# Thirteen late input blocks per layer split into two rounded halves, and the gate tables dealt out anew

## The reference

```
q = (h @ wq).reshape(B, S, H, PEER_QDIM)
s1, s2 = the two halves of q against k1, k2        # 128 scores each
v1, i1 = lax.top_k(s1, K);  v2, i2 = lax.top_k(s2, K)
top_s, pos = lax.top_k(v1 + v2 of all pairs, K)
gates = jax.nn.softmax(top_s, axis=-1)
act = jax.nn.gelu(jnp.einsum('td,tkd->tk', xc, u[ec]), approximate=False)
y = jnp.einsum('tk,tkd->td', act * gc, v[ec])
```

## Time and profile before

| | |
|---|---|
| median of three executions | 1907.43 us (1905.97 to 1910.97) |
| the profiled execution | 1905.52 us |
| its span, first to last instruction | 1903.6 us |
| mean granted TensorE clock in it | 0.997 |
| TensorE, VectorE, ScalarE, GpSimd busy | 98%, 83%, 52%, 23% of the span |
| DMA | 547.98 MB, mean 288 GB/s |

### The profile page before, as it was taken

One profiled execution on the slowest core, in us unless ns is written; L12 is line 12 of the kernel. 1 busy time (PEld: TensorE's weight loads), 2 busy tenths in 40 slices (PEclk: granted clock), 3 DMA queues, 4 the chain that ended last, 5 costly groups with the idle time before them and its releaser, 6 DMA issues.

```text
span 1903.6 us, 35537 instructions
## 1 busy us (share of the span) xinstructions
PE 1859.9 (98%) x13294; PEld 1803.7 (95%) x13294; DVE 1587.8 (83%) x3192; ACT 989.2 (52%) x1933; POOL 438.6 (23%) x368
## 2 busy tenths in 40 slices
PE   6999999999999999999999999999999999999998
PEld 6899989999999999999988898999999999999998
DVE  7788889989688598898888978898976776888897
ACT  4478455621455455555555775555115554555554
POOL 0000000022455334333100001000226552334330
PEclk9999999999999999999999999999999999999999
DMA  8766765699989899999867746656998888999994
GB/s 340 251 247 214 277 213 185 203 323 362 318 311 336 302 343 358 346 352 346 309 238 265 257 161 211 229 189 220 361 359 275 300 297 303 349 347 356 350 354 157
DMA packets 152160, 547.98 MB, mean 288 GB/s; under 512 B 18080, under 2 KB 18720, under 8 KB 151520
## 3 DMA queue, kind: packets, MB, share of 16 engines
q1 hardware_dynamic: 115168, 412.08, 61.0%
q0 software_dynamic: 36864, 134.23, 19.8%
HBM read 540.74 MB, written 1.57 MB: 285 GB/s over the span
## 4 chain that ended last, share of the span: by engine, by line
PE 74%; DVE 13%; DMA 7%; ACT 3%; issue 2%; POOL 1%; SPq 0%; ACTq 0%; DVEq 0%
PE ps L1717 24%; PE ps L2023 13%; PE ps L2019 9%; PE ps L1601 5%; DVE w_lo L1008 4%; DMA raw<-in_v 4%; PE ps L1597 3%; PE ps L1598 3%; PE ps L1594 3%; PE ps L1988 2%; PE ps L1759 1%; ACT w_hi L651 1%; DMA raw<-in_u 1%; DVE big L1474 1%; PE ps L1915 1%
## 5 line engine op out<-in xcount | busy, mean ns | idle before, releaser
L651 ACT CAST w_hi<-raw 128x1024 fp32r<-128x1024 f32 x460 | 483.6, 1051 | 516.0 <-PE ps L2019 163.1
L1008 DVE TENSOR_TENSOR w_lo<-raw,w_hi 128x1024 fp32r<-128x1024 f32 x460 | 562.2, 1223 | 121.3 <-ACT w_hi L651 118.9
L1717 PE MATMUL ps<-big,raw 128*128 128x192 f32 x3104 | 516.7, 327 | 0.6 <-DMA raw<-in_u 0.5
L1717 PEld LDWEIGHTS ps<-big,raw 128*128 128x128 f32 x3104 | 502.9, 190 | 1.8 <-DMA raw<-in_u 1.6
L614 POOL DMA_INDIRECT hot<-in_v,spare x128 | 199.4, 1558 | 365.5 <-DVE big L1474 314.7
L2023 PE MATMUL ps<-h_both,w_hi 128*128 128x384 f32 x960 | 191.4, 341 | 0.6 <-ACT w_hi L651 0.5
L2023 PE MATMUL ps<-p_both,w_hi 128*128 128x384 f32 x960 | 191.0, 340 | 0.3 <-ACT w_hi L651 0.3
L2023 PEld LDWEIGHTS ps<-h_both,w_hi 128*128 128x128 f32 x960 | 162.9, 189 | 1.6 <-issue 1.0
L2023 PEld LDWEIGHTS ps<-p_both,w_hi 128*128 128x128 f32 x960 | 162.8, 189 | 0.6 <-ACT w_hi L651 0.5
L1597 PE MATMUL ps<-h_both,w_hi 128*128 128x256 f32 (+1 forms) x648 | 160.3, 286 | 1.4 <-ACT big L656 1.2
L1474 DVE SCALAR_TENSOR_TENSOR big<-hot,spare,big 128x1024 f32<-128x1024 f32 x126 | 161.1, 1278 | 0.0
(11 more groups left out here) (247 smaller groups left out, 2918.9 us busy)
## 6 DMA issues: line engine op xcount, KB each, us to landing
raw<-in_u SPq DMA_DIRECT2D x256, 512.0 KB, 5.0
raw<-in_v SPq DMA_DIRECT2D x256, 512.0 KB, 6.2
raw<-in_win SPq DMA_DIRECT2D x104, 512.0 KB, 4.6
hot<-in_ada SPq DMA_DIRECT2D x62, 512.0 KB, 4.9
big<-in_ada SPq DMA_DIRECT2D x34, 512.0 KB, 7.4
raw<-in_wq SPq DMA_DIRECT2D x32, 512.0 KB, 5.0
raw<-in_wout SPq DMA_DIRECT2D x16, 512.0 KB, 4.5
big<-in_decay SPq DMA_DIRECT2D x2, 1536.0 KB, 8.0
```

The source lines that it names most:

```text
L651: nc.scalar.copy(w_hi[:, j % 2, :], raw[:, j, :]).then_inc(hi_ready, covered(n))
L1008: tt(w_lo[:, j % 2, :], raw[:, j, :], w_hi[:, j % 2, :].bitcast(F32), ALU.subtract).then_inc(lo_ready, covered(n))
L1717: last = mm(bank(E[m % 2])[:, 0:DENSE], raw[:, j, P * k:P * (k + 1)], h_full[:, k, :], start=(k == 0), stop=(k == KC - 1))
```

## The change

Of the plain blocks 98 to 127 every second one from 98 to 122 (`LATE_U`, 13 per layer, 26 in all) is now split. Its high part goes to bank 6 or 7, and its low half is added by one matmul at the end of the plain block that follows. The Gelu of a late block runs after the next block is done, together with that block's own, and so the two products of VectorE stand together. Plain blocks among them use banks 1 and 0 in turn. Apart from that, GpSimd makes 3 of the 8 tables of each gate, ScalarE 3 and VectorE 2, at all 24 gates of a layer.

```diff
--- before.py
+++ after.py
@@ -92,7 +92,7 @@
 V_COPIES = 5
 SWAPS = 4
 BATCH = 8
-POOL_TOK, ACT_TOK = 2, 4
+POOL_TOK, ACT_TOK = 3, 3
 GATE_SCALE = 1024.0
 N_SPARSE = 64
 DENSE = SEQ - N_SPARSE
@@ -153,7 +153,9 @@
 PLAIN_U = range(N_HALF, N_U)
 assert len(FIRST_U) % LONG == 1 and LONG % 4 == 0 and N_HALF % 4 == 3
 V_PLAIN = 2
-RAW = LIFTED | {N_BLOCKS * l + B_U + m for l in range(DEPTH) for m in range(N_HALF, N_U + V_PLAIN)}
+LATE_U = range(98, 124, 2)
+LATE_BANK, MIXED_BANK = (6, 7), (1, 0)
+RAW = LIFTED | {N_BLOCKS * l + B_U + m for l in range(DEPTH) for m in range(N_HALF, N_U + V_PLAIN) if m not in LATE_U}
 V_PAIRS = (N_V - V_PLAIN) // 2
 EU = (1, 6, 7, 0)
 
@@ -437,6 +439,16 @@
         def home(m):
 
             return (M if m < 2 or C_AQ <= m < C_AQ + 2 else E)[m % 2]
+
+        def late_bank(m):
+
+            return bank(LATE_BANK[m // 2 % 2])
+
+        def plain_bank(m):
+
+            if LATE_U[0] < m <= LATE_U[-1] + 1:
+                return bank(MIXED_BANK[m // 2 % 2])
+            return bank(E[(m + (m > LATE_U[-1])) % 2])
         block = ctx.enter_context(nc.Block())
 
         @block.sync
@@ -949,18 +961,24 @@
                     if n + 2 not in RAW:
                         round_hi(n + 2, (n + 2) % RING)
                     act.wait_ge(block_done, n + 1)
+                    if m in LATE_U:
+                        nc.scalar.copy(p_both[:, 1, 0:1, 0:nd], late_bank(m)[:, nd:2 * nd]).then_inc(ulow_copied, 1)
                     if m in FIRST_U:
                         nc.scalar.copy(p_both[:, 1, m % 2, 0:nd], bank(EU[m % 4])[:, nd:2 * nd]).then_inc(ulow_copied, 1)
                     if m - 1 in FIRST_U:
                         nc.scalar.activation(acts[:, m - 1:m, 0:nd], bank(EU[(m - 1) % 4])[:, 0:nd], ACT.Gelu).then_inc(out_taken, 1)
+                    if m - 1 in LATE_U:
+                        act.wait_ge(producted, l * N_PROD + m - M_PROD - 2)
+                        nc.scalar.activation(acted[:, (m - 1) % 2:(m - 1) % 2 + 1, 0:nd], late_bank(m - 1)[:, 0:nd], ACT.Gelu
+                                             ).then_inc(out_taken, 1)
                     if m < M_PROD:
                         o = acts[:, m:m + 1, 0:nd]
                     else:
-                        if m >= M_PROD + 2:
+                        if m >= M_PROD + 2 and m not in LATE_U:
                             act.wait_ge(producted, l * N_PROD + m - M_PROD - 1)
                         o = acted[:, m % 2:m % 2 + 1, 0:nd]
-                    if m not in FIRST_U:
-                        nc.scalar.activation(o, bank(E[m % 2])[:, 0:nd], ACT.Gelu).then_inc(out_taken, 1)
+                    if m not in FIRST_U and m not in LATE_U:
+                        nc.scalar.activation(o, plain_bank(m)[:, 0:nd], ACT.Gelu).then_inc(out_taken, 1)
                     if m == 2:
                         copy_scores(3)
                     if m in (TOK_COPY_AT, TOK_COPY_AT + 1):
@@ -1512,9 +1530,10 @@
                         us.link(stt(gate16[:, 0, :], turned_gate, GATE_SCALE, gate16[:, 1, :], ALU.mult, ALU.subtract))
                         ts(neg[:], rt[:, 2, 0:DENSE].rearrange("p (b t) -> p b t", t=BATCH)[:, :, POOL_TOK:POOL_TOK + ACT_TOK], -2.0, None,
                            ALU.mult).then_inc(choices_ready, 1)
-                    if m > M_PROD:
-                        product(m - 1, weighed)
-                        products += 1
+                    for at in (m - 2, m - 1):
+                        if at >= M_PROD and m == (at + 2 if at in LATE_U else at + 1):
+                            product(at, weighed)
+                            products += 1
                     for b in range(N_GATE):
                         if gate_after(b) == m - 1:
                             weigh(b, products)
@@ -1703,7 +1722,7 @@
                     last = mm(o[:, 0:DENSE], w_lo[:, s, P * k:P * (k + 1)], h_hi[:, k, 0:DENSE], start=False, stop=False,
                               skip_group_check=True)
                 if after_wide:
-                    pe.wait_ge(ulow_copied, l * len(FIRST_U) + m - FIRST_U[0])
+                    pe.wait_ge(ulow_copied, l * (len(FIRST_U) + len(LATE_U)) + m - FIRST_U[0])
                     last = add_half(j - 1)
                 last.then_inc(block_done, 1)
 
@@ -1714,7 +1733,7 @@
                 pe.wait_ge(raw_in[j], (n - j) * (16 // RING) + 16)
                 pe.wait_ge(out_taken, l * EV + E_U + m - behind + 1)
                 for k in range(KC):
-                    last = mm(bank(E[m % 2])[:, 0:DENSE], raw[:, j, P * k:P * (k + 1)], h_full[:, k, :], start=(k == 0),
+                    last = mm(plain_bank(m)[:, 0:DENSE], raw[:, j, P * k:P * (k + 1)], h_full[:, k, :], start=(k == 0),
                               stop=(k == KC - 1))
                 if then:
                     last = then()
@@ -1990,13 +2009,39 @@
 
                 def last_half():
 
-                    pe.wait_ge(ulow_copied, (l + 1) * len(FIRST_U))
+                    pe.wait_ge(ulow_copied, l * (len(FIRST_U) + len(LATE_U)) + len(FIRST_U))
                     return add_half(FIRST_U[-1])
+
+                def late_half(m):
+
+                    pe.wait_ge(ulow_copied, l * (len(FIRST_U) + len(LATE_U)) + len(FIRST_U) + LATE_U.index(m) + 1)
+                    return mm(late_bank(m)[:, 0:DENSE], ident_r, p_both[:, 1, 0, 0:DENSE], start=False, stop=True,
+                              skip_group_check=True)
+
+                def project_late(m):
+
+                    s, n = m % 2, l * N_BLOCKS + B_U + m
+                    pe.wait_ge(hi_ready, n + 1)
+                    pe.wait_ge(out_taken, l * EV + E_U + m - 3)
+                    o = late_bank(m)
+                    for k in range(KC):
+                        mm(o[:, 0:2 * DENSE].rearrange("p (a t) -> p a t", a=2), w_hi[:, s, P * k:P * (k + 1)],
+                           h_both[:, :, k, 0:DENSE], start=(k == 0), stop=False, skip_group_check=True)
+                    pe.wait_ge(lo_ready, n + 1)
+                    for k in range(KC):
+                        last = mm(o[:, 0:DENSE], w_lo[:, s, P * k:P * (k + 1)], h_hi[:, k, 0:DENSE], start=False, stop=False,
+                                  skip_group_check=True)
+                    last.then_inc(block_done, 1)
 
                 pe.wait_ge(hfull_ready, KC * (l + 1))
                 for m in PLAIN_U:
                     behind = m - FIRST_U[-1]
-                    project_plain(l, m, 3 if behind < 3 else 2, last_half if behind == 1 else None)
+                    if m in LATE_U:
+                        project_late(m)
+                    elif m - 1 in LATE_U:
+                        project_plain(l, m, 4, lambda: late_half(m - 1))
+                    else:
+                        project_plain(l, m, 3 if behind < 3 else 2, last_half if behind == 1 else None)
                     if m == TURN_AT:
                         pe.wait_ge(gates_ready, l + 1)
                         pe.wait_ge(score_copied, 8 * (l + 1))
```

## The result

The changed kernel takes 1914.82 us (median of 10 runs, 1906.84 to 1920.26), the kernel before 1906.51 us (median of 10, 1901.55 to 1910.97). The ratio is 1.0038, with a 95% interval of 1.0024 to 1.0052, so 4.6 to 9.9 us more. The forecast was 1904.0 us, in a range of 1900.5 to 1912. What came out is the case that had been given 0.14: GpSimd starved, about 1915 us. Its profiled execution, the slowest of the ten, took 1920.26 us with a span of 1918.5.

What follows compares the result with a forecast made beforehand. TensorE, busy for all 79.30 us of the touched stretch, was taken as the bound. -5.5 + 1.6 + 0.5 = -3.4 us took the profiled 1905.5 to 1902.1; 1.9 us more for the median gave 1904.0 us, range 1900.5 to 1912.

Steps and rivals of the forecast that it cites:

- GpSimd starved: Rival: GpSimd's third table falls into VectorE's dot or low half, rows land late; +7.9 us, about 1915 us, chance 0.14.
- TensorE's gain: Late blocks on TensorE: each split block saves 0.21 us, 26 save 5.5 us.
- ScalarE's cost of nothing: ScalarE's rounding, copy and three tables per round finish before the late block ends; cost nothing.
- The first gate: First gate of each layer: a third GpSimd table delays it 0.78 us, twice, taken as 1.6 us.
- GpSimd: 13 tables at 0.80 bring it to about 51 of 76.6 us ... I cost both at nothing: Late stretch: GpSimd's added tables and later fetches, and DMA moving the same bytes, cost nothing.
- The sum: All terms over the whole kernel: -5.5 + 1.6 + 0.5 = -3.4 us.
- The 2.78 us of the first table: GpSimd's first table before the first gate took 2.78 us, the others 0.80 each; a third was priced at 0.78.
- the second rival: GpSimd's queue in the late stretch: up to 1.15 us waiting per blocked item, 0.9 us lag a round; +7.9 us, chance 0.14.
- GpSimd waits and VectorE does not: Where GpSimd tables overlap VectorE dots, only GpSimd is delayed, so the sum needs no term for VectorE.
- VectorE falls behind by 2.2 to 3.3 us, against 2.8 us of cover ... I take 0.5: Layer 0's late stretch: VectorE's work exceeds 76.6 us, so TensorE loses 0 to 0.5 us at the last late blocks.
- the low half's cover: VectorE's low half is ready about 2.3 us after the previous late block, needed at 5.1, leaving 2.8 us.
- its own argument against it: Against GpSimd starving: GpSimd is busy half of the time now and its lead is over a gate.

Runs made afterwards that it cites:

- e1: Changed kernel with the tables dealt out as before (GpSimd 2, ScalarE 4, VectorE 2), so late blocks alone; 1903.57 us, 0.9997 of the kernel before.
- e6: Changed kernel with GpSimd's third table only filled with zeros, reading nothing; 1900.86 us, 0.9974 of the kernel before.
- e7: Changed kernel with GpSimd's tables of each gate put behind the fetch due in the same two steps; 1912.07 us, 1.0028 of the kernel before.

## Why the prediction was wrong

*TensorE's gain* was right, and so was ScalarE's cost of nothing: in the late stretch TensorE never waited for the rounded half or the copy. Undisturbed, the stretch is 2.40 us shorter per layer and gate 0 to gate 11 another 0.3, 5.4 us in all, against 5.5.

*The first gate* was right: 1.15 us of waiting instead of 0.39, 1.5 us for both layers against 1.6.

*"GpSimd: 13 tables at 0.80 bring it to about 51 of 76.6 us ... I cost both at nothing"* is the step that failed. It took 69 and 73 us of 82 and 79. The sum priced a table at what it takes when nobody is in its way, though the earlier trace rows showed one at 1.87 us behind a dot. The late blocks add 1.2 us of two-input work a round to VectorE, for which GpSimd's tables and fetches wait: e1 shows 8 to 10 us from that alone, and the third table has to fit into what is left. GpSimd was then late with the rows (in the late stretches of the first profile VectorE's dots waited 3.5 and 5.6 us for them), not with its own tables, of which only the first gates show a wait.

The rows had one more sign. The 2.78 us of the first table, read as a property of the first, were the same wait. VectorE at that moment, in the kernel before:

```profile
499.80 1.21 DVE L1455 CUSTOM_DVE_ANT_0 big<-big 128x1024 f32<-128x1024 f32 x1
...
500.94 1.22 DVE L1455 CUSTOM_DVE_ANT_0 big<-big 128x1024 f32<-128x1024 f32 x1
```

The table began at 499.98, inside the first dot, and ended at 502.75, 0.6 us after the second. In layer 1 it was the same. So a table could wait for two dots in a row, and the price of a blocked table was up to 2.0 us and not the 1.15 of the second rival.

*"GpSimd waits and VectorE does not"* failed too. It rested on one dot that began 0.18 us before a table's end, and the earlier trace rows spoke against it: the longest low half, 1749 ns instead of 1221, is one of two that ran beside additions on GpSimd in the kernel before:

```profile
966.63 3.37 POOL L605 TENSOR_TENSOR big<-big 128x256 f32<-128x256 f32 x3 [42.24 <-ACT big L688]
...
967.67 3.42 DVE L1008 TENSOR_TENSOR w_lo<-raw,w_hi 128x1024 fp32r<-128x1024 f32 x2
```

In the changed kernel the product at 0.63 us and the one-hot table at 0.99 us show VectorE waiting. In the stretch, its one-hot tables took 0.79 us on average in layer 0 instead of 0.69, its products 0.38 instead of 0.36. Over all its instructions of the stretch that is 2.2 us in layer 0 and 1.9 in layer 1, against their medians in the kernel before. The rule of the Trainium skill ("SBUF — State Buffer", "Who interferes with whom") that was set aside says that the exclusion works in both directions. This case's trace now agrees with it at 580.51. At 604.11 it agrees in part only, since there the one-hot table lost 0.31 us beside a GpSimd table of 0.79 us and didn't wait for its end. It also says that a GpSimd instruction that only writes isn't held up by a VectorE one with two SBUF inputs; the 194 to 196 ns of e6's fills agree.

*"VectorE falls behind by 2.2 to 3.3 us, against 2.8 us of cover ... I take 0.5"* was mis-sized. e1 measures 2.75 us in layer 0. The direction was right, and layer 1 lost nothing. The cover was the wrong one. The low half had 2.8 us, but the tables for the next gate, further back in the same queue, had 2.4 us, and TensorE waited at gates only. The prediction did name the 2.4 us, and then treated them as if the lag ended at the low half's cover. A modulation reduction, 1.15 us in one step, stands ahead of those tables, and the four late gates of e1 are behind such steps.

*The forecast as a whole.* -5.4 + 1.5 and, as measured in the two profiles, 10.6 to 13.4 us of waits (5.2 to 8.0 more from gate 0 to gate 23, and the 5.4 that were saved), against 0.5. That makes +6.7 to +9.5 us, and the medians say 4.6 to 9.9. The rival that named the mechanism priced it at +7.9 us and got 0.14 of the chances. It should have had more: its own argument against it, GpSimd busy for half the time, was a share taken while VectorE was idle for 19 and 25% of the stretch. That its price comes so close is in part luck: it has no term for VectorE's own lag (2.75 us in e1) or for its lengthened instructions, and a blocked table can cost more than it allowed.

Left open: how much of the loss is VectorE's lengthened instructions and how much is the late rows. Only e7 speaks to it, in layer 1: there VectorE's instructions were lengthened by 3.2 us in all, more than the 1.9 us of the changed kernel, and TensorE lost only 0.6 us. For layer 0 no run separates them.

## What to carry to other kernels

Before work is given to GpSimd, count not its idle time but the time in which VectorE runs nothing with two SBUF inputs, since GpSimd's reading instructions waited for those here. GpSimd, idle for half of the stretch before, was busy for 84 and 92% of it once VectorE went from 80 and 74% to 93 and 91% and a third table was added. When several things wait in one queue, take the smallest cover of all of them, and go on to the gate behind it. Two changes that cost little each (0.9997 and 1.0016 here, 1.0013 together if they added up) can cost more together (1.0038) if they use the same slack. And look up the longest instruction of a group, not only the median: the 2.78 us and the 1749 ns stood in the rows.

## What was unexpected in the hardware's behaviour

A GpSimd table instruction of 0.78 us took up to 3.95 us while VectorE ran a dot, a low half and a dot without a break. In the changed kernel, GpSimd and then VectorE:

```profile
644.89 3.95 POOL L636 TENSOR_SCALAR hot<-con,rt 128x128 f32<-128x128 f32 x1
```

```profile
644.83 1.22 DVE L1473 CUSTOM_DVE_ANT_0 big<-big 128x1024 f32<-128x1024 f32 x1
...
645.97 1.22 DVE L1026 TENSOR_TENSOR w_lo<-raw,w_hi 128x1024 fp32r<-128x1024 f32 x1
647.11 1.22 DVE L1473 CUSTOM_DVE_ANT_0 hot<-hot,big 128x1024 f32<-128x1024 f32 x1
```

The change from one VectorE instruction to the next did not let GpSimd in, twice running. An indirect DMA issue of GpSimd was lengthened in the same way, from 0.94 to 1.99 us in the late stretch, and to as much as 2.04 us for such rows in the kernel before. VectorE's tables with one input (L1421) were lengthened too, in some cases from 0.34 to 0.69 us. ScalarE's tables, which run beside VectorE all the time, kept their length: the squares took 0.386 to 0.405 us and the relus 0.477 to 0.497 in all 144 cases.
